# Near bias of group A added by VectorE in short tiles only, GpSimd's splits in halves behind each combination, reciprocal spread against ones in PSUM

## What is computed

```python
def probs(qb, k):
    s = jnp.einsum('bqhd,bkhd->bhqk', qb, k).astype(jnp.float32) * scale + bias
    s = jnp.where(allowed, s, -jnp.inf)
    return jax.nn.softmax(s, axis=-1)
p = probs(qb1, k1) - lam * probs(qb2, k2)
return jnp.einsum('bhqk,bkhd->bqhd', p.astype(v.dtype), v)
...
s = jnp.where(valid[:, None], s + bias, -jnp.inf)
p = jax.nn.softmax(s, axis=-1)
return jnp.einsum('bhqk,bqkhd->bqhd', p.astype(v.dtype), vg)
...
y = jnp.einsum('bse,ed->bsd', jnp.concatenate([ao, bo], axis=-1), w_out)
return x + y
```

## Time and profile before

| what | value |
|---|---|
| median of 3 runs | 738.67 us (737.96 to 740.0) |
| the profiled execution | 737.92 us, span 736.1 us |
| PE busy | 714.5 us, 97% of the span |
| DVE busy | 615.0 us, 84% |
| POOL busy | 363.1 us, 49% |
| ACT busy | 321.6 us, 44% |
| TensorE clock granted | 0.998 of full speed over the run |

### The profile page before, as it was taken

One profiled execution on the slowest core, in us unless ns is written; L12 is line 12 of the kernel. 1 busy time (PEld: TensorE's weight loads), 2 busy tenths in 40 slices (PEclk: granted clock), 3 DMA queues, 4 the chain that ended last, 5 costly groups with the idle time before them and its releaser, 6 DMA issues.

```text
span 736.1 us, 12004 instructions
## 1 busy us (share of the span) xinstructions
PE 714.5 (97%) x4112; PEld 592.7 (81%) x4112; DVE 615.0 (84%) x1351; ACT 321.6 (44%) x723; POOL 363.1 (49%) x445
## 2 busy tenths in 40 slices
PE   8999999999999899999999999999999999999996
PEld 7757888888888788888888888888787878788886
DVE  5578999999998889888699999999789888546554
ACT  7547131131313666666631131314877767522222
POOL 5220222223556769771135654546999999612210
PEclk9999999999999999999999999999999999999999
DMA  7351211211220010213021112130010122313231
GB/s 282 108 145 46 52 49 44 57 44 46 66 76 1 0 44 1 51 31 101 16 71 45 43 44 57 44 87 0 30 45 11 50 55 91 116 58 100 73 115 57
DMA packets 25140, 45.10 MB, mean 61 GB/s; under 512 B 3140, under 2 KB 11512, under 8 KB 24952
## 3 DMA queue, kind: packets, MB, share of 16 engines
q1 hardware_dynamic: 23912, 43.28, 20.2%
q10 hardware_dynamic: 1168, 1.05, 0.4%
HBM read 35.92 MB, written 6.57 MB: 58 GB/s over the span
## 4 chain that ended last, share of the span: by engine, by line
PE 51%; DVE 23%; POOL 18%; issue 4%; ACT 2%; DMA 2%; POOLq 0%; SPq 0%; ACTq 0%; DVEq 0%
PE psum L1288 24%; PE psum L1509 12%; DVE score L1655 10%; DVE top L1650 10%; POOL k_high_twice L628 3%; PE psum L1383 2%; PE psum L1371 2%; PE psum L1208 2%; PE psum L1180 2%; POOL qT_r L631 2%; POOL k_zero_low L631 2%; POOL q_low_high L631 2%; POOL kT_r L631 2%; POOL near_low L769 2%; PE psum L1349 2%
## 5 line engine op out<-in xcount | busy, mean ns | idle before, releaser
L624 POOL TENSOR_TENSOR w_lo<-w_raw,w_hi 128x512 fp32r<-128x512 f32 x60 | 77.5, 1294 | 214.7 <-ACT w_hi L822 214.4
L1655 DVE MATCH_REPLACE8 score<-top,score 128x640 f32<-128x640 f32 (+5 forms) x176 | 157.4, 908 | 0.0
L1650 DVE MAX8 top<-score 128x8 f32<-128x640 f32 (+5 forms) x176 | 148.7, 911 | 1.2
L822 ACT ACTIVATE w_hi<-w_raw 128x512 fp32r<-128x512 f32 x60 | 37.4, 629 | 209.8 <-PE psum L1288 206.8
L998 ACT ACTIVATE probs<-psum,small 128x384 f32<-128x384 f32 (+7 forms) x128 | 94.6, 740 | 39.5 <-DVE small L1748 38.0
L1288 PE MATMUL psum<-big_hi,w_hi 128*128 128x512 f32 x256 | 99.7, 389 | 0.0
L1288 PE MATMUL psum<-big_hi,w_lo 128*128 128x512 f32 x256 | 99.6, 389 | 0.0
L1288 PE MATMUL psum<-big_lo,w_hi 128*128 128x512 f32 x256 | 99.6, 389 | 0.0
L1288 PE MATMUL psum<-w_hi,big_hi 128*128 128x512 f32 x192 | 74.7, 389 | 0.0
L1288 PE MATMUL psum<-w_lo,big_hi 128*128 128x512 f32 x192 | 74.7, 389 | 0.0
L1288 PE MATMUL psum<-w_hi,big_lo 128*128 128x512 f32 x192 | 74.7, 389 | 0.0
(11 more groups left out here) (199 smaller groups left out, 1608.8 us busy)
## 6 DMA issues: line engine op xcount, KB each, us to landing
w_raw<-in_w_in SPq DMA_DIRECT2D x62, 256.0 KB, 2.7
xs<-in_x SPq DMA_DIRECT2D x8, 512.0 KB, 6.5
k_high_twice<-k_high_twice SPq DMA_DIRECT2D x16, 256.0 KB, 3.7
xres<-in_x SPq DMA_DIRECT2D x8, 512.0 KB, 4.8
out_y<-y_out SPq DMA_DIRECT2D x8, 384.0 KB, 2.9
w_tail<-in_w_out SPq DMA_DIRECT2D x10, 256.0 KB, 2.6
bias_scratch<-bias_row SPq DMA_DIRECT2D x1, 2304.0 KB
bias<-bias_scratch SPq DMA_DIRECT2D x12, 128.0 KB, 3.1
```

Of the source, the lines that this page charges most:

```text
L624: pool.tensor_tensor(lo[:, 0:cols], w_staged(n)[:, 0:cols], hi[:, 0:cols].bitcast(f32), ALU.subtract).then_inc(w_lo_made, 1)
L822: act.activation(w_parts(n)[0][:, 0:cols], w_staged(n)[:, 0:cols], ACT.Copy).then_inc(w_hi_made, 1)
L1650: ins = dve.max(top8[:, i - SEL0, :], sc)
L1655: ins = dve.match_replace(sc, top8[:, i - SEL0, :], sc, TAKEN)
```

## The change

Three edits. First, in phase A both maps get the near bias by PE's products where the tile is long, and both by `soften` on DVE where it is short (before, map 0 always by products and map 1 always by `soften`). The mask of the last head's bias is set one place later. Second, POOL's splits are cut in two (`steps`): the first three instructions in one step, the last two in the next, so that a block's four parts are spread over 8 steps (4 to 11 and 12 to 19, and for block 1 the keys over 0 to 3) where they lay in 4 (5 to 8 and 13 to 16, and 0 and 1), and each piece waits until DVE has combined step s + 2. Third, `share` multiplies the reciprocals by ones in PSUM where it copied them in SBUF.

```diff
+        def bias_by_product(i):
+
+            return i >= HALF // P
...
-            def split_k(ph, b, half):
+            def split_k(ph, b, half, steps=(0, 1)):
...
+                if 0 in steps:
+                    link(rounded(k0[0:HEAD, c], kT[0:HEAD, b, c]))
+                    link(rounded(k1[HEAD:P, c], kT[HEAD:P, b, c]))
+                    link(rest(k1_low[b % 2][HEAD:P, c], kT[HEAD:P, b, c], k1[HEAD:P, c]))
+                if 1 in steps:
+                    link(rest(kT_r[0:HEAD, b, c], kT[0:HEAD, b, c], k0[0:HEAD, c]))
+                    ins = pool.memset(kT_r[HEAD:P, b, c].bitcast(f32), 0.0)
+                    if half == 1:
+                        ins.then_inc(kh_made, 1)
...
-                ahead = s + 3
-                if s < 2 or ahead >= TILES and ahead % TILES < 4 and ahead < 3 * TILES:
+                ahead = s + 4
+                if s < 4 or ahead >= TILES and ahead < 3 * TILES:
                     pool.wait_ge(o_gated, s + 1)
-                if s < 2:
-                    split_part(0, 1, s + 2)
-                elif ahead >= TILES and ahead % TILES < 4 and ahead < 3 * TILES:
-                    split_part(0, ahead // TILES + 1, ahead % TILES)
+                    pool.wait_ge(combined, s + 3)
+                if s < 4:
+                    split_part(0, 1, 2 + s // 2, (s % 2,))
+                elif ahead >= TILES and ahead < 3 * TILES:
+                    split_part(0, ahead // TILES + 1, ahead % TILES // 2, (ahead % 2,))
...
-                    banded = ph == 0 and m == 0 and near < c + w
+                    banded = ph == 0 and bias_by_product(i) and near < c + w
...
-                if ph == 0 and m == 0:
+                if ph == 0 and bias_by_product(i):
...
+            def first_min(s, m):
+
+                far_min(0, s, m)
+                if not bias_by_product(place_of(0, s)[1]):
+                    soften(0, s, m)
...
+            ones = bank(BACK_BANK)[:, P:2 * P]
...
-                dve.tensor_copy(shares[:, :, :], rinv[:, c:c + 2].unsqueeze(2).broadcast_to([P, 2, HEAD])
-                                ).then_inc(shares_made, 1)
+                dve.tensor_tensor(shares[:, :, :], ones.rearrange("p (m d) -> p m d", m=2),
+                                  rinv[:, c:c + 2].unsqueeze(2).broadcast_to([P, 2, HEAD]), ALU.mult
+                                  ).then_inc(shares_made, 1)
...
+            link(dve.memset(ones, 1.0))
```

More of the change, by code:

```diff
@@ L631, in rest, with split_q @@
                 return pool.tensor_tensor(out, src, high.bitcast(f32), ALU.subtract)
-            def split_q(ph, b, half):
+            def split_q(ph, b, half, steps=(0, 1)):
                 c = slice(half * HALF, (half + 1) * HALF)
@@ L637, in split_q @@
                 part = q_part[:, :] if b == 0 else k0[0:HEAD, c]
[L638 to L647, removed]
@@ L649, in split_k @@
-            def split_k(ph, b, half):
+                if 0 in steps:
+                    link(rounded(q1[HEAD:P, c], qT[HEAD:P, b, c]))
+                    link(rest(q1[0:HEAD, c], qT[HEAD:P, b, c], q1[HEAD:P, c]))
+                    link(rounded(part, qT[0:HEAD, b, c]))
+                if 1 in steps:
+                    link(rest(qT_r[HEAD:P, b, c], qT[0:HEAD, b, c], part))
+                    ins = rounded(qT_r[0:HEAD, b, c], qT[0:HEAD, b, c])
+                    if half == 1:
+                        ins.then_inc(split, 1)
+                        pool.wait_ge(split, ph * BLOCKS + b + 1)
+                    else:
+                        link(ins)
@@ L651, in split_k @@
+            def split_k(ph, b, half, steps=(0, 1)):
                 c = slice(half * HALF, (half + 1) * HALF)
                 _, k0, k1 = stacks[ph][b % 2]
[L653 to L664, removed]
+                if 0 in steps:
+                    link(rounded(k0[0:HEAD, c], kT[0:HEAD, b, c]))
+                    link(rounded(k1[HEAD:P, c], kT[HEAD:P, b, c]))
+                    link(rest(k1_low[b % 2][HEAD:P, c], kT[HEAD:P, b, c], k1[HEAD:P, c]))
+                if 1 in steps:
+                    link(rest(kT_r[0:HEAD, b, c], kT[0:HEAD, b, c], k0[0:HEAD, c]))
+                    ins = pool.memset(kT_r[HEAD:P, b, c].bitcast(f32), 0.0)
+                    if half == 1:
+                        ins.then_inc(kh_made, 1)
+                        pool.wait_ge(kh_made, ph * BLOCKS + b + 1)
+                    else:
+                        link(ins)
@@ L666, in split_part @@
+            def split_part(ph, b, j, steps=(0, 1)):
                 if j == 0 and b == 1:
                     wait_chunk_used(pool, (A_GROUPS, B_GROUPS)[ph][-1] * DB + DB - 1)
-                elif j == 0:
+                elif j == 0 and 0 in steps:
                     pool.wait_ge(s_ready, units_before(ph, b - 1))
-                (split_q, split_q, split_k, split_k)[j](ph, b, j % 2)
+                (split_q, split_q, split_k, split_k)[j](ph, b, j % 2, steps)
             def project_low(ph):
@@ L1800, in _ @@
             select(1, TILES - 2, TILES - 1)
-            far_min(0, 0, 0)
-            far_min(0, 0, 1)
-            soften(0, 0, 1)
+            first_min(0, 0)
+            first_min(0, 1)
             for s in range(STEPS):
@@ L1806, in _ @@
                     finishA(s - 2)
+                if s == 3 * TILES - 1:
+                    dve.wait_ge(bias_kept[1], 16)
+                    link(dve.memset(near_high[0:CHUNK, 0, BAND - CHUNK:BAND], MASKED))
                 if s + 1 < STEPS:
-                    far_min(0, s + 1, 0)
+                    first_min(s + 1, 0)
                 invert(0, s)
@@ L1811, in _ @@
                 combine(s)
-                if s == 3 * TILES - 2:
-                    dve.wait_ge(bias_kept[1], 16)
-                    link(dve.memset(near_high[0:CHUNK, 0, BAND - CHUNK:BAND], MASKED))
                 if s + 1 < STEPS:
-                    far_min(0, s + 1, 1)
-                    soften(0, s + 1, 1)
+                    first_min(s + 1, 1)
             finishA(STEPS - 2)
```

## The result

| | before | after |
|---|---|---|
| median | 738.32 us (737.86 to 740.0, 4 runs) | 750.39 us (747.89 to 751.91, 4 runs) |
| the profiled execution | 737.92 us, span 736.1 | 751.91 us, span 750.1 |
| clock granted over the run | 0.998 | 0.984 |

The ratio is 1.0151, with a 95% interval of 1.0127 to 1.0174. The forecast was 741.5 us, with a range of 737.0 to 745.5: the direction was right, and the size far too small.

The account below looks back on a forecast made before the run. PE and DVE were taken to bound phase A, POOL phase B. Edges 10.0, relief -4.8, near bias -1.0 and spread -0.9 sum to +3.3 us: 741.2 or 742.0 by base, forecast 741.5, range 737.0 to 745.5.

Parts of the forecast that it names:

- Sum of the edges: Starts of blocks 1 to 3 in phase A: PE waits for key copies, +10.0 us, bounds 7.9 and 13.
- relief: Phase A: DVE's combinations meet fewer of POOL's splits in their new place, -4.8 us, between -3 and -6.3.
- The path with the chunk in it: Block 2's edge: a weight chunk waiting for ACT precedes the last keys; first product 8.0 us behind the combination, 4.0 late.
- The combinations of blocks 1 and 2 below 6 us for six each: Sign in phase A: DVE's six combinations total below 6 us per block, where they took 8.67 and 8.24.
- 63%: Share of the combinations' excess time that came through in block 1's stretch, 2.13 of 3.36 us; used to size the relief.
- Near bias -1.0: Phase A: DVE saves time in long tiles, loses some in short ones; -1.0 us, bounds 0 and -4.2.
- Spread -0.9: Phase B: cheaper copies save DVE some 8 us, but the phase hangs on POOL; -0.9 us, between 0 and -3.
- its two small gains: Spread term, phase B: POOL no longer stands behind a copy, 0.5 us, and block 3 of the phase, 0.4 us.
- The three waits for copies: Sign in phase A: PE shows three waits of 2.5 to 4.5 us, the middle longest, where there was none.
- Block 1's stretch: Sign in phase A: first product to step-13 combination near 25 us, was 27.28; 23 would mean near bias is worth more.
- POOL falls behind: Rival: chunks and waits leave POOL a step late, edges cost 13 us or more; 743 to 746 us, chance 17%.
- a fixed cost of 2 us: Skill's DMA figure for the key copies, against the row's 3.9; an edge would be up to 1.9 us cheaper.

Follow-up runs that it names:

- The turns: Changed kernel with 30 transposes of the unit matrix on PE ahead of the first product of blocks 1 to 3 in phase A: 743.77 us, ratio 1.0069.
- the control: Kernel before the change, with ten transposes of the unit matrix ahead of the first product of blocks 1 to 3: 742.45 us, ratio 1.0050.
- the run without the wait: Changed kernel without GpSimd's wait for the combination ahead of each split piece, its other waits kept: 746.87 us, ratio 1.0115.
- with ten turns: Changed kernel with ten transposes of the unit matrix on PE ahead of the first product of blocks 1 to 3: 744.80 us, ratio 1.0101.
- those splits alone: Kernel before the change with only the splits edit, each piece one step earlier than in the changed kernel, without the near bias: 738.87 us, ratio 1.0008.

## Why the prediction was right in direction and wrong in size

**The step that failed is one that is missing from the sum.** "Sum of the edges: 3.0 + 4.0 + 3.0 = +10.0 us" prices an idle PE by its idle time alone. What PE did right behind each edge was priced at the clock of the kernel before. It ran at 1.2 GHz for 15.2 us there, which cost 6.6 us. The turns show it: with 30 of them the edges stay, the clock and 6.6 us come back, and in the control, where the clock is whole, turns gain nothing. By the profiled executions, whose spans are 14.0 us apart, the whole account is: edges +9.9, clock in the stretches +6.5 (84.97 - 78.45), relief of both edits in phase A -2.7 (what is left over), phase B and what follows +0.3. The forecast's sum was +3.3 us, 10.7 too little: 6.5 for the clock, 3.1 for the relief and 1.2 for phase B and the rest, less 0.1 for the edges.

**The edges were right.** 3.2, 2.9 and 3.8 us against 3.0, 4.0 and 3.0; the sum 9.9 against 10.0. Singly two were off. The middle one was not the longest: its combination was itself late (1.84 us beside the chunk, 300.96 to 302.80), the chunk had begun at 300.99, ahead of its end and not behind it, and so only a gate stood between. The path with the chunk in it, 8.0 us, is what the run without the wait shows, 8.14. The third was longer by 0.8 us; there SP issued the second copy 0.9 us behind the first in place of 0.5, which is half of it.

**The relief was mis-sized.** "-4.8 us", with -1.0 for the near bias, was 5.8 us in phase A. With the clock held, the stretches are 78.4 us where they were 80.6, and phase A ends 6.7 us later with edges 9.3 us longer: 2.6 us of relief for both edits. Three parts of that step were wrong. (1) The forecast counted combinations only. They gave 4.3 us (35.7 to 31.4), but with the clock held the factors took 1.4 us back (10.5 to 11.8): a one-column DVE instruction in SBUF is held up by GpSimd just like a long one. (2) "The combinations of blocks 1 and 2 below 6 us for six each" held for block 1 (5.7) and not for block 2 (6.7), where the chunk of weights remained. (3) Of what DVE is spared, about half comes through, not 63%: against the kernel with the near bias alone, combinations and factors save 47.7 - 43.3 = 4.4 us, and phase A, less its longer edges (10.0), 2.2 us.

**Near bias -1.0:** 1.0 us at the end of phase A alone, 1.1 on top of the splits; the medians say 0.6 and 0.9, and the interval of the run alone doesn't tell it from nothing. The term was right as far as can be told. But on top of the splits one step earlier it is worth 738.9 - 735.5 = 3.4 us (with the spread, which alone gave nothing), and 4.3 at the end of phase A (366.7 - 362.4), about the upper bound of 4.2. Its worth depends on where the pieces fall. One microsecond of it can be named: without the near bias edit the combination of step 13 began at 297.79 beside the chunk (from 297.77) and took 1.81 us, with it 0.75. The rest was not settled.

**Spread -0.9:** nothing, the upper bound. The reason given for a small value (phase B hangs on GpSimd) held; its two small gains did not appear.

**The signs.** The three waits for copies (3.5, 4.2, 4.1 us) and 0.291 us for the spread came as written. Block 1's stretch "near 25 us" was 29.2, and 26.7 with the clock held: 2.4 us of the miss are the clock, the rest the relief. Of the rivals, *POOL falls behind* came nearest with 743 to 746, still below the 750.4, and its reason did not occur: the last piece of a block began 0.14 to 0.4 us behind the combination that it waited for. (Beside that rival stands a fixed cost of 2 us. The section of the Trainium skill that the forecast names there, "Anatomy of one DMA", gives it for transfers that GpSimd issues; these are issued by SP, and the copies landed after 3.6 us in the median, so it was right to go by the row.)

Left open is what exactly takes the clock away. It fell after 1.90 us of idle time in one run and not after 2.12; with ten turns it fell at an idle time of 2.93 us and not at 2.25 and 2.76. The lower clock lasted 5.8 and 6.0 us behind two edges of the changed kernel and 3.4 behind the middle one, whose wait was the longest. The length of the wait alone does not explain this.

## What to carry to other kernels

A wait that is put into TensorE's queue is to be priced twice, for its length and for what stands behind it, since the engine may come back at half its clock; and if it can't be avoided, harmless matmuls in the idle time buy the second part back. Where there was no idle time to hold them, they cost 4 us. A piece of work that is moved should keep the distance that its whole chain needs (here rest, clearing, two copies and landing, 6.3 us against the 3.5 us that an edge had), and one step decided between 1.5% slower and 0.4% faster. When two engines hold each other up, sum all instructions of the held engine and not the one in which it was seen first, because a shift moves the cost to its neighbours.

## What the hardware showed that was not expected

TensorE's granted clock fell from 1.00 to 0.50, from 2.4 to 1.2 GHz, at idle times of 3.5, 4.2 and 4.1 us in an otherwise full queue, and stayed there for 5.8, 3.4 and 6.0 us behind them although the engine was busy again at once; a 512-column matmul took 0.63 us in place of 0.40. The Trainium skill (TensorE: Matmul & The Clock Gate, section "What's actually happening") says that a gate sets the clock by how busy the array has recently been. The trace agrees, with its 0.50 behind each of the three gaps. The forecast should have put this rule to the waits that it added.

The turns of the unit matrix kept the clock up: 30 of them in the gap, and 1.00 behind it. The same page (section "Part 4: PE-mode transpose") says that the full clock does not engage for transposes. Here the measurement decides: for these turns of 32-bit data, with other matmuls on both sides, it stayed engaged. The profile records them as MATMUL and doesn't show whether they ran in the mode that the page means.

DVE and GpSimd held each other up in instructions of a single column too: the 32 factors took between 10.5 and 13.7 us in phase A, depending on where GpSimd's pieces lay. A free one took 0.22 us, which is 7.0 for 32. Two of them from the kernel with those splits alone, and GpSimd beside the first:
```profile
284.19 1.06 DVE L1779 SCALAR_TENSOR_TENSOR small<-small 128x1 f32<-128x1 f32 x1
...
289.64 0.22 DVE L1779 SCALAR_TENSOR_TENSOR small<-small 128x1 f32<-128x1 f32 x1
```
```profile
283.94 1.29 POOL L631 TENSOR_TENSOR k_zero_low<-kT,k_high_twice 64x512 fp32r<-64x512 f32 x1
```
The factor began 0.25 us behind GpSimd's instruction and ended with it, at 285.25 and 285.23. It is the picture of the earlier trace rows with one column in place of 128.
